# One more plain block of up products ahead of the first gates, one less behind them, and two memory groups a block later, in a two-layer float32 kernel on one Trainium2 core

## The reference

```python
z = h @ w_in                                  # a, g, q, k, v and the forget logits
mem_n = rms_norm(mem, norm_memkv)             # the memory rows, normed
k = (mem_n @ w_mk)...; v = (mem_n @ w_mv)...
...
# the expert layer of the second block, 128 x 128 = 16384 experts
s = jnp.einsum('thsd,hskd->thsk', q, sub_keys)          # scores of 2 x 128 keys, 8 heads
v_half, i_half = lax.top_k(s, 16)
best, pos = lax.top_k(sums of the two halves' values, 16)
experts = i1 * 128 + i2
gates = softmax(best)
act = gelu(x . u[expert]) * gates
out = sum of act * v[expert]
```

## Time and profile before

| what | value |
|---|---|
| median of 3 runs | 1404.82 us (1404.79 to 1405.01) |
| the profiled execution's own time | 1404.95 us |
| its span (first to last instruction) | 1403.2 us |
| PE busy | 1387.3 us (99%) |
| PEld busy | 1232.1 us (88%) |
| DVE busy | 1067.6 us (76%) |
| ACT busy | 793.2 us (57%) |
| mean granted clock of PE | 0.999 |

### The profile page before, as it was taken

The page is one execution under the profiler, slowest core; times in us unless marked ns, Lnnn a source line. Parts: engine busy times, 40 slices in busy tenths (PEclk is TensorE's granted clock), DMA queues, the critical chain, the costliest instruction groups (busy, mean ns, idle before and its releaser), DMA issues.

```text
span 1403.2 us, 26201 instructions
## 1 busy us (share of the span) xinstructions
PE 1387.3 (99%) x8842; PEld 1232.1 (88%) x8842; DVE 1067.6 (76%) x1902; ACT 793.2 (57%) x1291; POOL 66.4 (5%) x64
## 2 busy tenths in 40 slices
PE   8999999999999999999999999999999999999998
PEld 8988988888898888899999999888888888888886
DVE  7997786666697687699999996666666666677776
ACT  6776865554776445545655555555555555555554
POOL 1100000000011421100000000000000000000000
PEclk9999999999999999999999999999999999999999
DMA  8544355555345424644557788557566575667753
GB/s 300 193 127 148 119 168 181 195 193 183 132 158 176 133 91 137 218 157 165 202 188 252 278 279 272 184 194 253 183 214 232 186 252 190 210 232 254 250 194 146
DMA packets 103241, 274.37 MB, mean 196 GB/s; under 512 B 8336, under 2 KB 40832, under 8 KB 102672
## 3 DMA queue, kind: packets, MB, share of 16 engines
q1 hardware_dynamic: 65600, 238.21, 49.8%
q10 hardware_dynamic: 37232, 33.32, 7.5%
q0 software_dynamic: 352, 2.11, 0.5%
HBM read 254.67 MB, written 18.87 MB: 195 GB/s over the span
## 4 chain that ended last, share of the span: by engine, by line
PE 94%; DVE 4%; ACT 1%; issue 0%; DMA 0%; POOL 0%; POOLq 0%; ACTq 0%
PE Y L2208 46%; PE AO L2208 44%; PE M L2208 3%; DVE CV L1282 1%; DVE wl L1152 1%; ACT wh L538 0%; PE M L2604 0%; DMA X<-in_x 0%; PE M L2298 0%; PE Y L2447 0%; DVE xn L1182 0%; POOL wl L2093 0%; ACT junk L760 0%; ACT junk L567 0%; PE Y L2318 0%
## 5 line engine op out<-in xcount | busy, mean ns | idle before, releaser
L1152 DVE TENSOR_TENSOR wl<-raw,wh 128x1024 fp32r<-128x1024 f32 x439 | 543.4, 1242 | 182.5 <-ACT wh L538 181.7
L2208 PE MATMUL AO<-xhl,wh 128*128 128x256 f32 (+3 forms) x2784 | 648.0, 315 | 1.6 <-DVE wl L1152 0.9
L538 ACT CAST wh<-raw 128x1024 fp32r<-128x1024 f32 x439 | 460.0, 1050 | 140.4 <-PE Y L2208 71.8
L2208 PEld LDWEIGHTS AO<-xhl,wh 128*128 128x128 f32 x2784 | 455.4, 188 | 33.3 <-DVE wl L1152 1.3
L2208 PE MATMUL AO<-xhl,wl 128*128 128x256 f32 (+2 forms) x1776 | 484.7, 282 | 0.0
L2208 PEld LDWEIGHTS AO<-xhl,wl 128*128 128x128 f32 x1776 | 334.1, 188 | 7.9
L2208 PE MATMUL Y<-wh,peer_al 128*128 128x512 f32 x512 | 199.3, 389 | 0.0
L2208 PE MATMUL Y<-wl,peer_ah 128*128 128x512 f32 x512 | 199.3, 389 | 0.0
L2208 PE MATMUL Y<-wh,peer_ah 128*128 128x512 f32 x512 | 199.2, 389 | 0.0
L1037 ACT CAST peer_ah<-hid 128x256 fp32r (+1 forms) x128 | 52.0, 406 | 177.5 <-DVE hid L1949 92.6
L2208 PEld LDWEIGHTS Y<-wl,peer_ah 128*128 128x128 f32 x512 | 96.1, 188 | 20.2
(11 more groups left out here) (388 smaller groups left out, 1592.5 us busy)
## 6 DMA issues: line engine op xcount, KB each, us to landing
raw<-in_stream SPq DMA_DIRECT2D x440, 512.0 KB, 3.3
gate_spill<-gstage ACTq DMA_DIRECT2D x32, 512.0 KB, 3.2
gates<-gate_spill ACTq DMA_DIRECT2D x6, 2048.0 KB, 15.3
gates<-gate_spill ACTq DMA_DIRECT2D x6, 512.0 KB, 6.7
rowg<-in_post SPq DMA_DIRECT2D x3, 512.0 KB, 4.3
X<-in_x SPq DMA_DIRECT2D x2, 512.0 KB, 4.7
memx<-in_mem SPq DMA_DIRECT2D x1, 1024.0 KB, 7.8
keys<-in_keys POOLq DMA_DIRECT2D x1, 1024.0 KB, 7.1
```

The source lines that it names most:

```text
L538: nc.scalar.copy(wh[:, s, :], raw[:, s, :]).then_inc(split_hi, 1)
L1152: nc.vector.tensor_tensor(wl[:, s, :], raw[:, s, :], wh[:, s, :].bitcast(F32), ALU.subtract)\
L2208: return nc.tensor.matmul(o, a, b, start=start, stop=stop)
```

## The change

It has two parts that do not touch each other. In the stage "qk" the third and fourth memory groups (g = 2, 3) stand behind blocks 5 and 6 in place of 4 and 5, on ACT, DVE and PE. In the expert layer `PLAIN` goes from 29 to 30 and `FIRST_TURN` stays 28, so the turned picks stand where they stood, block 29 becomes a plain one, rounds 0 to 31 carry blocks 30 to 61, and blocks 62 and 63 are left behind them. DVE's loop over these last blocks is stretched by one step that makes no split, so that it still copies two rounds from `gstage`.

```diff
-PLAIN = 29
+PLAIN = 30
...
-FIRST_TURN = PLAIN - 1
+FIRST_TURN = PLAIN - 2
...
+        MEM_AT = {2: 0, 3: 1, 5: 2, 6: 3}
...
@@ ACT, DVE and PE, stage "qk" @@
-                if 2 <= j < 6:
-                    mem_part(j - 2)
+                if j in MEM_AT:
+                    mem_part(MEM_AT[j])
...
@@ DVE, behind the rounds @@
-            for c in range(PLAIN + BATCHES, AHEAD - 1):
-                split(P0 + 4, c)
+            for c in range(PLAIN + BATCHES, AHEAD):
+                if c < AHEAD - 1:
+                    split(P0 + 4, c)
                 if c < PLAIN + BATCHES + 2:
                     b = c - PLAIN - 2
                     dve.wait_ge(g_out, b + 1)
```

## The result

The changed kernel takes 1407.94 us in the median of 17 runs (1405.88 to 1408.68), the kernel before 1404.93 (1404.79 to 1406.71): ratio 1.0017 [1.0009, 1.0024], slower by 0.17% (the two medians alone differ by 0.21%). Its times fall into two groups, 6 runs at 1405.9 to 1406.7 and 11 at 1407.8 to 1408.7. The profiled execution is one of the lower group, with a time of its own of 1406.04; before's was 1404.95. So there are two losses to explain: 1.1 us that the trace shows, and about 1.9 us more that some executions have.

What follows compares the result with a forecast made beforehand. PE bounds the kernel, 94% of the chain, so only its waits can pay. Gains of 0.09 (memory groups) and 0.22 (plain block) sum to 0.31 us, giving 1404.5 us on the median's scale, range 1403.5 to 1405.5.

Steps and rivals of the forecast that it cites:

- the landing of the last part: Behind round 31: the gates' last transfer, issued at 864.38, lands 5.9 us later, at 870.28.
- The price of a late landing: First down block: 0.53 us of new wait on `peer_al`; each microsecond beyond 5.9 is one on PE.
- rival of the other side: Last part's transfer lands late beside stream loads; slower above 6.2 us, 1405.3 at 6.7; chance 0.15.
- The size of the loss: Whole kernel: slower than before by more than 0.2%, above 1407.6 us; chance 0.02.
- the clock: PE's mean granted clock is 0.999 over the span; nothing put down for it, stalls being under 1 us.
- The memory groups: Stage "qk": the stall goes from `ml` to `FA`, a wait of 0.37 us; 0.09 gained of 0.46.
- The gates: Ahead of the first gates: wait on `spread` goes, 0.75 us won there; no new wait in the rounds.
- Everything is recovered: Rival: last part lands in 5.4 us or less and `FA` passes in time; up to 1.21 won, 1403.6; chance 0.17.
- both covers: The slack ahead of the products of `FA` and of the last part's transfer; called small.
- the two stalls: PE's waits on `ml` (0.46 us) and `spread` (0.75 us); together 1.21, all the change can win.
- Both stalls only move: Rival: `FA` takes the first gain, a landing near 6.1 us takes 0.75; no difference, 1404.8; chance 0.20.
- theory C: Experiments' theory: waiting at the first down block makes TensorE's granted clock fall in some executions, giving times near 1408.

Runs made afterwards that it cites:

- e2: Kernel before with only the change's memory groups moved, PLAIN staying 29: 1404.98 us, ratio 1.0.
- h1: Changed kernel with the last turn of TensorE's dense feed-forward loop written out, 116 instructions more ahead of the gates: 1404.83 us, ratio 0.9999.
- h3: Changed kernel with the last turn of TensorE's xbc loop written out, 192 instructions more ahead of the gates: 1404.94 us, ratio 1.0.
- g1: Changed kernel with two turns of TensorE's dense feed-forward loop written out, 232 instructions more: 1404.93 us, ratio 1.0.
- f3: Changed kernel with the last part fetched a round earlier and DVE's forget-gate operations set ahead of the memory group: 1403.82 us, ratio 0.9992.
- i2: Changed kernel with the last part's two transfers issued behind the last plain block's activation: 1409.66 us, ratio 1.0033.
- e1: Changed kernel unaltered, run again: 1406.39 us, ratio 1.0015.
- e3: Kernel before with only the change's plain block (PLAIN 30), memory groups where they were: 1406.43 us, ratio 1.0013.
- f4: Changed kernel unaltered, for one more profile: 1406.28 us, ratio 1.001.
- g2: Changed kernel with one turn of TensorE's feed-forward loop and two of its xbc loop written out, 500 instructions more: 1406.61 us, ratio 1.0016.
- g3: Changed kernel unaltered, one more profiled execution: 1406.57 us.
- h4: Changed kernel unaltered, run beside the kernels with loop turns written out: 1407.90 us, ratio 1.0018.
- i1: Changed kernel with 13 transposes that nobody reads on TensorE, filling the wait ahead of the first down block: 1406.52 us, ratio 1.0011.
- e4: Changed kernel with the last part of gates fetched a round earlier: 1404.26 us, ratio 0.9994.
- h2: Kernel before with the last turns of TensorE's feed-forward and xbc loops written out, 308 instructions more: 1405.10 us, ratio 1.0001.
- f1: Changed kernel with 154 already met waits (77 instructions) ahead of TensorE's first transposes: 1412.97 us.
- i3: Changed kernel with the last part issued behind the last plain block's activation and 44 unread transposes filling TensorE's wait: 1409.06 us, ratio 1.0029.

## Why the prediction was wrong

**The step that failed** is the landing of the last part: "Now it lands at 864.38 + 5.9 = 870.28". It takes 7.2 us there. The 5.9 was read from the transfer in its old place, and I took it along to the new one as if it were the transfer's own. It holds (5.9 or 6.0) in every kernel in which the part goes out right behind the store and no fetch of code lies between issue and landing, and in none in which one does. The price of a late landing was right: 0.5 us of wait at 5.9, one more for each microsecond, hence 0.53 + 1.3 = 1.8 us; the profile prints 1.71. Against before's own 1404.95 the sum is then 0.31 less and 1.3 more, 1405.9; the profiled execution took 1406.04. The working had this as its rival of the other side, at 0.15, but bounded it at 6.7 us by the median of other transfers; nothing there was a bound on what one engine can be held up by. The size of the loss was set too low with it: over 0.2%, 1407.6 and more, had 0.02, and the median is 1407.94.

**The second error** is that nothing was put down for the clock, "the stalls that go or come are all under 1 us". With the longer landing the new stall was 1.7, and in more than half of the 17 runs something cost 1.9 us more. What cost it stays open: a wait of 3.4 us costs 1.6 us in clock, which is near that, but no fall of the clock behind the wait of 1.7 was seen in any of the five profiled executions of this kernel.

**What held.** The memory groups: no wait on `ml`, one of 0.20 on `FA` as the profile prints it, and 0.37 as forecast from start to start (55.38 + 0.44 = 55.82 to 56.19), 0.04 us gained by themselves in `e2`, forecast 0.09, neither of which the medians can tell from nothing. The gates: the wait on `spread` is gone, no wait in the rounds. With the packet of code elsewhere (`h1`, `h3`, `g1`) the change gives 1404.83, 1404.94 and 1404.93 against 1404.92 to 1404.97, where 0.31 less was forecast. These times lie inside the range of 1403.5 to 1405.5, but so would those of a change that does nothing: the medians show a gain of 0.09 us at most, which cannot be told from zero. The profiled execution of `h1` had 1404.67, 0.28 below before's.

**The rivals.** "Everything is recovered" needs both covers back; `f3` puts them back and takes 1403.82, 1.13 us under its before, of the 1.21 that the two stalls held. Its times (1403.67 to 1403.91) lie below all of before's there (1404.75 to 1405.23), while the ratio's interval just touches 1. No run here has a landing as short as the 2.9 us that the prediction estimated from the fit of the Trainium skill (page "DMA: Bandwidth & Descriptors", section "Anatomy of one DMA"); the shortest seen is 4.5 us (`i2`). "Both stalls only move" is what `h1` comes to in its median.

**Open.** Which executions fall into the upper group. It was seen in 30 of 71 runs of the kernels in which the packet hits the part (after, `e1`, `e3`, `f4`, `g2`, `g3`, `h4`) and in none of 33 of `h1`, `h3` and `g1`; the share differs much between the chips used (7 of 11 for `h4`, none of 9 for `f4`), and no profiled execution was one. The clock readings and the price are in keeping with theory C, the one time in `i1` is against it; a landing that is later still in these runs would explain both, since it would make a wait longer than the 13 transposes. Neither was seen. One of before's first 17 times is 1406.71, 1.8 us above their median, and none of its other 126 is over 1405.29; what that one was is open too. Why the part lands in 4.5 us when it is issued 5 us behind the store was not tried either.

## What to carry to other kernels

A transfer's time from issue to landing belongs to its place too, not to the transfer alone: when an edit moves its issue and its cover is thin, look at every queue that is served in the new stretch, the one for instructions too, and give the term a bound that one late DMA engine can reach. Moving blocks between a loop and straight code moves the places at which an engine fetches its program; that moves other transfers' landings by a microsecond, and the next edit elsewhere can bring it back, so the robust mend is to give the transfer its cover again (`e4`), not to shift the code. Read the granted clock of every run, not only of the profiled one, when times come in two groups.

## What the runs showed of the hardware

One packet of 16 KB for TensorE's code takes 0.92 us of one DMA engine's time (0.8% of 16 engines over 7.2 us; 1.2 in `h2`) and, served while a transfer of 384 KB is under way, makes that land 0.8 to 1.6 us later. An instruction with two waits that are already met takes 108 ns on TensorE (`f1`: 8.31 us for 77). A wait of TensorE of 3.4 us was followed by some 3 us at the lower clock (granted 0.50), 1.7 us of clock in all (`i2`); with the wait filled the clock stayed at 1.00 (`i3`). The first of the two DMAs landed in 5.9 us when issued 0.4 us behind a store on its queue, and in 4.5 us when issued 5 us behind it (`i2`).
